# Rounding buffers of low weights moved one word off a 16-byte line, those of high weights kept on it

## What is computed

```
h = causal_dwconv(x @ w_up, conv_w, conv_b)
gate, up = jnp.split(h, 2, axis=-1)
return (jax.nn.gelu(gate) * up) @ w_down
```

## Time and profile before

| | us |
|---|---|
| median of 3 runs | 3287.39 |
| lowest and highest of them | 3285.52 to 3289.57 |
| span of the profiled execution | 3284.6 |
| TensorE busy with matmuls | 3232.2 |
| TensorE's weight loads | 2855.1 |
| VectorE busy | 2195.8 |
| ScalarE busy | 1667.5 |
| GpSimd busy | 24.5 |

### The profile page before, as it was taken

One profiled execution on the slowest core, in us unless ns is written; L12 is line 12 of the kernel. 1 busy time (PEld: TensorE's weight loads), 2 busy tenths in 40 slices (PEclk: granted clock), 3 DMA queues, 4 the chain that ended last, 5 costly groups with the idle time before them and its releaser, 6 DMA issues.

```text
span 3284.6 us, 53186 instructions
## 1 busy us (share of the span) xinstructions
PE 3232.2 (98%) x21672; PEld 2855.1 (87%) x21672; DVE 2195.8 (67%) x2836; ACT 1667.5 (51%) x2138; POOL 24.5 (1%) x38
## 2 busy tenths in 40 slices
PE   9999999999999999999999999999999999999998
PEld 8888898888888888888888888888888888888887
DVE  6577767666676456676766666745675767647676
ACT  5574346555554335554555555533564456444563
POOL 0000000000000000011000000000000000000000
PEclk9999999999999999999999999999999999999999
DMA  7352145455444554534445445455544434444342
GB/s 279 143 210 67 57 167 200 181 188 196 179 185 175 184 190 183 190 119 180 164 181 199 182 186 198 159 186 192 188 168 185 171 129 167 186 175 167 129 171 112
DMA packets 47254, 563.64 MB, mean 172 GB/s; under 512 B 5072, under 2 KB 7264, under 8 KB 10720
## 3 DMA queue, kind: packets, MB, share of 16 engines
q1 hardware_dynamic: 47072, 561.06, 45.4%
HBM read 558.92 MB, written 2.12 MB: 171 GB/s over the span
## 4 chain that ended last, share of the span: by engine, by line
PE 90%; DVE 5%; ACT 3%; issue 2%; DMA 0%; SPq 0%; DVEq 0%; ACTq 0%
PE bank L863 40%; PE bank L849 21%; PE bank L968 10%; PE bank L973 5%; PE bank L1002 3%; ACT spl_r L1771 1%; PE bank L1468 1%; DVE ring L2506 1%; PE bank L784 1%; PE bank L788 1%; PE bank L782 1%; DVE spl_r L2506 1%; DVE xb L2506 1%; DVE xa L2506 0%; DVE scr L2506 0%
## 5 line engine op out<-in xcount | busy, mean ns | idle before, releaser
L2506 DVE TENSOR_TENSOR spl_r<-ring,spl_r 128x2048 fp32r<-128x2048 f32 (+2 forms) x429 | 961.3, 2242 | 485.8 <-ACT spl_r L1771 480.8
L863 PE MATMUL bank<-all_r,spl_r 128*128 128x512 f32 x4960 | 1196.6, 393 | 3.2 <-ACT spl_r L1771 3.2
L1771 ACT ACTIVATE spl_r<-ring 128x2048 fp32r<-128x2048 f32 x407 | 779.2, 1915 | 591.0 <-PE bank L849 484.1
L863 PEld LDWEIGHTS bank<-all_r,spl_r 128*128 128x128 f32 x4960 | 914.5, 188 | 189.5 <-issue 8.0
L849 PEld LDWEIGHTS bank<-all_r,spl_r 128*128 128x128 f32 x5008 | 642.1, 191 | 24.2
L849 PE MATMUL bank<-all_r,spl_r 128*128 128x256 f32 x5008 | 650.0, 283 | 0.0
L2506 DVE TENSOR_TENSOR dsp_r<-ring,dsp_r 128x1408 fp32r<-128x1408 f32 x126 | 204.8, 1625 | 206.4 <-ACT dsp_r L1771 206.2
L968 PE MATMUL bank<-scr_r,dsp_r 128*128 128x512 f32 x1386 | 338.8, 392 | 0.0
L1771 ACT ACTIVATE dsp_r<-ring 128x1408 fp32r<-128x1408 f32 x126 | 174.4, 1384 | 283.3 <-PE bank L973 283.1
L968 PEld LDWEIGHTS bank<-scr_r,dsp_r 128*128 128x128 f32 x1386 | 252.5, 189 | 47.4
L863 PE MATMUL bank<-scr_r,spl_r 128*128 128x512 f32 x1152 | 275.8, 391 | 2.9 <-ACT spl_r L1771 2.9
(11 more groups left out here) (437 smaller groups left out, 2673.9 us busy)
## 6 DMA issues: line engine op xcount, KB each, us to landing
ring<-in_up SPq DMA_DIRECT2D x88, 2048.0 KB, 7.8
ring<-in_down SPq DMA_DIRECT2D x64, 1408.0 KB, 6.0
ring<-in_ib SPq DMA_DIRECT2D x34, 2048.0 KB, 7.8
ring<-in_pg SPq DMA_DIRECT2D x16, 2048.0 KB, 7.8
ring<-in_out SPq DMA_DIRECT2D x16, 2048.0 KB, 7.9
ring<-in_in SPq DMA_DIRECT2D x12, 2048.0 KB, 7.7
ring<-in_ec SPq DMA_DIRECT2D x11, 2048.0 KB, 8.4
ring<-in_ea SPq DMA_DIRECT2D x8, 2048.0 KB, 10.5
```

The source lines that it names most:

```text
L863: mm(b[:, :], WHI[half][:, kk, :], pair(name, kk), start=kk == 0, stop=False, skip_group_check=True)
L1771: A(high[half], w[:, :, half * P:(half + 1) * P], ACT.Copy).then_inc(S["w_hi"], count)
L2506: return V.tensor_tensor(out, a, b, op)
```

## The change

The rounding buffers get 8 words of room each. The high ones still begin on a 16-byte line; the low ones begin one word after one. What follows them in the region moves by 32 words, and the views that share their space follow.

```diff
+HALF = 2048 + 8
+DOWN_HALF = FC * P + 8
+LOW_BEGIN = 1
+ROOM = 32
-SCR = 2 * (HHW + FC * 2 * P) - 2 * T
+SCR = 2 * (HHW + FC * 2 * P) - 2 * T + ROOM
...
-        scr_r, spl_r = named("scr_r", 2 * X, 2 * HHW, FR), named("spl_r", 2 * X + SPL, 8192, FR)
-        dsp_r = named("dsp_r", 2 * X + 2 * HHW, 4 * FC * P, FR)
+        scr_r, spl_r = named("scr_r", 2 * X, 2 * HHW, FR), named("spl_r", 2 * X + SPL, 4 * HALF, FR)
+        dsp_r = named("dsp_r", 2 * X + 2 * HHW, 4 * DOWN_HALF, FR)
...
-        all_r = named("all_r", 0, 2 * X + SCR, FR)
+        all_r = named("all_r", 0, 2 * X + SCR - ROOM, FR)
...
-        LG = scr[:, SPL + 4096:SPL + 6144].rearrange("p (k n) -> p k n", n=P)
+        LG = scr[:, SPL + 2 * HALF:SPL + 2 * HALF + 2048].rearrange("p (k n) -> p k n", n=P)
...
-        BF = [scr[:, SPL + 4096 * t:SPL + 4096 * t + 2048].rearrange("p (u x) -> p u x", u=16) for t in range(2)]
+        BF = [scr[:, SPL + 2 * HALF * t:SPL + 2 * HALF * t + 2048].rearrange("p (u x) -> p u x", u=16) for t in range(2)]
...
-        WHI, WLO = ([spl_r[:, 4096 * h + o:4096 * h + o + 2048].rearrange("p (k n) -> p k n", n=P)
-                     for h in range(2)] for o in (0, 2048))
-        DHI, DLO = ([dsp_r[:, FC * P * (2 * h + o):FC * P * (2 * h + o + 1)].rearrange("p (k n) -> p k n", n=P)
-                     for h in range(2)] for o in range(2))
+        def rounded_halves(tensor, room, n_tiles, low):
+            begins = [room * (2 * h + low) + LOW_BEGIN * low for h in range(2)]
+            return [tensor[:, b:b + n_tiles * P].rearrange("p (k n) -> p k n", n=P) for b in begins]
+        WHI, WLO = (rounded_halves(spl_r, HALF, DT, low) for low in range(2))
+        DHI, DLO = (rounded_halves(dsp_r, DOWN_HALF, FC, low) for low in range(2))
...
-            sp.dma_start(scr[:, SPL + 4096:SPL + 6144], dram["lg"][0]).then_inc(S["in_lg"], 16)
+            sp.dma_start(scr[:, SPL + 2 * HALF:SPL + 2 * HALF + 2048], dram["lg"][0]).then_inc(S["in_lg"], 16)
```

## The result

The changed kernel is slower: 3295.18 us (median of 7, 3293.64 to 3297.70) against 3287.27 us (median of 7) for the kernel before in the same comparison. The ratio is 1.0027, with a 95% interval from 1.0018 to 1.0037. The profiled execution's span is 3295.8 us, 11.2 us above the 3284.6 of before. Between the medians the difference is 7.9 us: the profiled execution of the changed kernel took 3297.67 us, nearly the longest of its seven.

What follows compares the result with a forecast made beforehand. TensorE's interval from one matmul to the next was taken to bound the kernel. Low-weight loads would save 6.3 x 7770 = 49 us, all else nothing: 3287.4 - 49 = 3238 us, range 3195 to 3312 us.

Steps and rivals of the forecast that it cites:

- What bounds the kernel: Whole kernel: time is the number of TensorE matmuls times the interval between them; only edits changing this interval show.
- the extra of 12.8 ns: TensorE, each full-rate matmul: time beyond its columns, taken as weight reads meeting the moving stream's reads.
- Part 2: Buffers that move by 16 words and stay on a line: cost nothing on either side.
- Part 3: VectorE's writes to low buffers one word off: at most 1% of 2.3 us, 0.02 us either way, hidden.
- Part 4: TensorE's low-weight loads one word off, beside 256-column matmuls: half the extra gone, 6.3 ns x 7770 = -49 us.
- the prediction's own sign: Line 849's sixteen low-weight matmuls: 1.80 to 1.86 us instead of 1.91; forecast wrong if their interval doesn't fall.
- stay too: 512-column matmuls with high weights: weights stay on lines, so their 228 ns stay.
- the sign that its mechanism is wrong: TensorE's intervals: mechanism wrong if the 512-column interval moves as much as the 256-column one.
- A: Rival, weight loads: fixed toll whatever the first address, +0 to +0.4 ns a load, 3287 to 3291 us; chance 0.30.
- B: Rival, low loads beside 256-column matmuls: second line read for some fetches, +50 us, 3337, or all, 3386; chance 0.25.
- C: Rival, low-weight matmuls: all of the extra goes, 109 ns, -82 us, 3205 us; chance 0.10 (-65 to -97 us).
- the range's lower end: Whole kernel: 3195 us, with half of the all-extra-gone case (0.05) said to lie below it.

Runs made afterwards that it cites:

- experiment 9: Changed kernel with high buffers at 0 of the 64 words and low buffers 19 words on instead of one: 3249.00 us, ratio 0.9884.
- experiment 1: Own kernel, matmuls alone, weights and moving operand at several words, regions placed unlike the full kernel: 3654 + 1886 ns with high and low at 0.
- experiment 5: Own kernel, matmuls alone, regions placed as in the full kernel, weights at 0 to 63 words: 3654 + 1913 ns with high and low at 0.
- experiment 12: Against the kernel before, to 64 words: only the second half's high buffer moved, 16 words, no buffer off a line: 3299.96 us, ratio 1.0038.
- experiment 11: Changed kernel with the second half's high buffer at 4160 instead of 4112, low buffers kept at 9 and 25 words: 3284.65 us, ratio 0.9992.
- experiment 3: Changed kernel with the high buffers one word past a line too: 3312.35 us, ratio 1.0074.
- Experiment 8: Changed kernel with both high buffers at 0 of the 64 words and both low ones at 1: 3281.90 us, ratio 0.9984.
- Experiment 7: Changed kernel with low buffers three words past a line instead of one, all else the same: 3306.20 us, ratio 1.0058.

## Why the prediction was wrong

- **What bounds the kernel:** right. TensorE's interval decides. Its busy time rose by 11.5 us with the span's 11.2, and fell by 39.3 with 35.8 in experiment 9, other engines unchanged.
- **Where the extra of 12.8 ns comes from:** supported, but not shown whole. Experiments 1 and 5 have it with every other engine idle, at the kernel's own 120.0 and 226.7 ns settled, so it is TensorE's own, and it changes with the place of either stream alone. That all of it is two reads meeting is not shown: no run streams without loading weights. The rule of the Trainium skill that I weighed ("TensorE: Matmul & The Clock Gate", "Step-by-step: what each phase is for": loading the next weights doesn't steal read bandwidth from the running matmul) does not hold for the time of these float32r matmuls: the place of the weights alone moved the settled interval between 113.3 and 122.2 ns.
- **Part 2, "moves by 16 words and stays on a line ...: cost nothing on either side, since their lines are whole before and after":** this step failed, and it turned the sign. Moving that buffer alone costs 12.4 us (experiment 12), and putting it back in the changed kernel brings 3295 to 3285 us (experiment 11, against 3295.18 in the first comparison). A high run goes from 3.65 to 3.73 us in every second half. I had taken the 16-byte line for the unit, from the description of the change and from the Trainium skill ("SBUF — State Buffer", "Specifications (TRN2)": its 16-byte lines); measured, the place repeats only after 64 words. The 120 ns that I cited for "any tile" in the buffers, "whatever the distance to the moving operand", held because every tile is 128 words and every buffer lay on a multiple of 128: no low or high buffer of before had ever left word 0 of the 64, and so the distance had never changed in what counts of it.
- **Part 3, VectorE's writes:** right, 2242 and 2244 ns. The prediction says the same of ScalarE and cites the earlier trace rows, which show VectorE alone; experiment 3 shows it for ScalarE's result, 1915 ns a half with the high buffer one word off and 1915 before.
- **Part 4, low loads one word off, -6.3 ns each and -49 us:** the sign is right for the word by itself, and the size was ten times too large. Experiment 8: low runs 1.91 to 1.89 us, 1.7 ns a load; the high runs that follow lose 8 ns of it, and each half piece of `down` loses 13 ns; -4.8 us in all (ratio 0.9984). In the changed kernel the low buffers lay at 9 and 25 words, not at 1, which gives no gain clear of the noise: experiment 11 has a ratio of 0.9992 (0.9983 to 1.0001). Low runs stayed at 1.90 and 1.92 us, by the prediction's own sign a wrong forecast. My reason, that 120 ns was the longest interval in the rows and so any shift would relieve it, was an argument from one place out of 64. The settled intervals at the others go from 113.3 to 122.2 ns, 44 of the 63 below 120, but a settled interval does not tell what a run of 16 takes.
- **High runs "stay too":** wrong, and they moved more than the low ones, which the prediction had named as the sign that its mechanism is wrong. A high run depends on its own place and on the low run ahead of it: with high kept at 0, low at 9 or 25 makes it 3.67 or 3.64 us. My reading is that the way in which two streams leave one run is how they enter the next; that is an argument from these lengths.
- **Rivals:** A's reason (the place doesn't matter) is refuted, and its time with it. B had the right sign, but its place and mechanism, a low load that needs more lines, are not what happened: low runs did not lengthen, and the loads beside them went from 191 to 188 ns on average. C was not a bad bound for what can be had: a run of low weights at 19 words takes 1.83 us, 114 ns a matmul, for -38 us where I had priced -82 for 109 ns.
- **The chances:** C was given -65 to -97 us, 3190 to 3222 us, so of its 0.10 far less than half lies below 3195; the range's lower end was worked out wrongly, without bearing on the outcome.

How the sum comes out: 3.684 us on average for undisturbed 512 runs of 16 against 3.654 is 0.030 us for some 387 halves (6192 low matmuls of line 849 by 16), 11.6 us, less some 1 us in the low runs, and 126 half pieces of `down` with 0.016 - 0.005 us, 1.4 us more. That is 12 us against a span that grew by 11.2, and medians that grew by 7.9.

What stays open: what in the chip has a turn of 64 words, and why one place settles at 113.3 and its neighbour at 118. The order over the 64 words is irregular, and I have no rule for it, only the table. The place of the weights isn't all of it either: with weights at 3 words runs of 512 columns settled at 230.0 ns in experiment 1 and 233.3 in experiment 5, with weights at 5 words runs of 256 at 119.8 and 116.7. The distance alone is not all either: with weights and moving operand both one word on, experiment 1 has 122.2 and 237.8 ns where both at 0 have 120.0 and 226.7.

## What to carry to other kernels

When TensorE's interval bounds a kernel and exceeds its columns, the distance from the moving operand to the weights, as it counts within 256 bytes, is a knob. Measure it with the kernel's own sequence of runs and nothing else, and with both operands at the kernel's own places: such a study of 1.8 ms gave 64 places at once, and where it had measured the very pair of places it forecast the full kernel's runs to a few ns. Experiment 7 failed where a number was carried to another place. A padding that only makes room for an idea is a change of its own: give it a run without the idea.

## What the runs showed of the hardware that I had not expected

- Float32r matmuls of 512 columns settled at 226.7 ns with weights at word 0 of 64, at 233.3 for 29 of the 64 places, and at 238.7 for the worst (word 41). With 256 columns they settled at 113.3 ns at words 13, 16, 19, 22 and 45, and 120.0 at word 0.
- Which place is best for a settled stream isn't what is best in short runs: word 16 settles at 113.3 ns, but 16 matmuls there between high runs take 1886 ns, at word 19 1827.
- The moving operand's place counts as well: weights at 0 and moving operand one word off settled at 123.3 ns for 256 columns and 236.7 for 512, three words off at 117.8 and 228.9 (experiment 1).
